# The second MLP's down products: three of four per slab by seven block products in place of eight, with the weight sums on GpSimd

## The reference, cut to what matters

```
def sqrelu_mlp(h, w1, w2):
    a = jax.nn.relu(h @ w1)          # h 256 x 2048, w1 2048 x 8192
    return (a * a) @ w2              # w2 8192 x 2048
...
x = x + mix                          # the S5 mixer with its gated output (tags gl, gg)
x = x + sqrelu_mlp(rmsnorm(x, norm_mlp[i]), mlp_w1[i], mlp_w2[i])
...
return rmsnorm(x, norm_final)
```

## Time and profile before

| | us |
|---|---|
| median of 3 runs | 2880.29 |
| lowest, highest | 2875.42, 2881.31 |
| span of the profiled execution | 2881.1 |
| PE busy in the span | 2841.2 |
| DVE busy | 1848.5 |
| ACT busy | 1408.0 |
| POOL busy | 374.1 |

### The profile page before, as it was taken

How to read it: one execution, slowest core, us unless ns; L and a number is a source line. 1 busy time by engine, 2 the same in 40 slices (tenths; PEclk the granted TensorE clock), 3 DMA queues, 4 the chain that set the end, 5 groups by cost and what they waited for, 6 DMA issues and landing times.

```text
span 2881.1 us, 46128 instructions
## 1 busy us (share of the span) xinstructions
PE 2841.2 (99%) x19454; PEld 2585.9 (90%) x19454; DVE 1848.5 (64%) x2543; ACT 1408.0 (49%) x1980; POOL 374.1 (13%) x420
## 2 busy tenths in 40 slices
PE   8999999999999999999999999989999999999998
PEld 8999988998899998999998899878889899988997
DVE  6998655776576665677665666677555555555555
ACT  5434645556555555444444445654545444444444
POOL 0000000000000000007883654122000000000000
PEclk9999999999999999999999999999999999999999
DMA  7555455552555555567776666586655555555553
GB/s 243 191 190 174 137 201 182 190 188 88 175 188 171 171 174 176 191 203 241 237 239 214 237 234 210 200 248 194 199 191 190 194 197 194 190 190 196 197 192 132
DMA packets 288047, 557.99 MB, mean 194 GB/s; under 512 B 25376, under 2 KB 35872, under 8 KB 287584
## 3 DMA queue, kind: packets, MB, share of 16 engines
q1 hardware_dynamic: 275328, 514.49, 54.3%
q0 software_dynamic: 5600, 22.78, 2.0%
q10 hardware_dynamic: 6912, 17.76, 1.8%
HBM read 530.87 MB, written 24.12 MB: 193 GB/s over the span
## 4 chain that ended last, share of the span: by engine, by line
PE 91%; DVE 4%; ACT 2%; DMA 1%; issue 1%; SPq 0%; ACTq 0%; POOL 0%; DVEq 0%
PE G L506 86%; PE T L506 3%; DVE WL L1714 1%; ACT WH L1103 1%; DVE Y L1722 1%; DMA FD<-s_k 1%; PE T L585 1%; DMA s_k<-VAR 1%; DVE XX L1714 0%; PE G L983 0%; ACT L1100 0%; ACT SC_e L1106 0%; DVE ZZ L2374 0%; DVE ST L1795 0%; DVE SC_e L1722 0%
## 5 line engine op out<-in xcount | busy, mean ns | idle before, releaser
L1714 DVE TENSOR_TENSOR WL<-RAW,WH 128x1024 fp32r<-128x1024 f32 (+1 forms) x948 | 1183.1, 1256 | 766.3 <-ACT WH L1103 756.6
L1103 ACT ACTIVATE WH<-RAW 128x1024 fp32r<-128x1024 f32 (+1 forms) x948 | 994.7, 1056 | 1027.7 <-PE G L506 1026.5
L506 PE MATMUL G<-A1h,WH 128*128 128x256 f32 (+1 forms) x2587 | 720.4, 280 | 3.1 <-DVE WL L1714 2.1
L506 PE MATMUL G<-A1l,WH 128*128 128x256 f32 x2560 | 712.9, 278 | 0.0
L506 PE MATMUL G<-A1h,WL 128*128 128x256 f32 x2560 | 711.5, 278 | 0.0
L506 PEld LDWEIGHTS G<-A1h,WH 128*128 128x128 f32 x2587 | 487.3, 189 | 7.0 <-DVE WL L1714 3.1
L506 PEld LDWEIGHTS G<-A1l,WH 128*128 128x128 f32 x2560 | 483.9, 189 | 0.4
L506 PEld LDWEIGHTS G<-A1h,WL 128*128 128x128 f32 x2560 | 482.9, 189 | 0.0
L506 PE MATMUL G<-WH,Bh 128*128 128x512 f32 x1024 | 399.3, 390 | 0.6 <-DVE WL L1714 0.6
L506 PE MATMUL G<-WH,Bl 128*128 128x512 f32 x1024 | 398.5, 389 | 0.0
L506 PE MATMUL G<-WL,Bh 128*128 128x512 f32 x1024 | 398.5, 389 | 0.0
(11 more groups left out here) (332 smaller groups left out, 3461.5 us busy)
## 6 DMA issues: line engine op xcount, KB each, us to landing
RAW<-in_mlp_w SPq DMA_DIRECT2D x256, 1024.0 KB, 5.3
RAW<-in_even_w_in SPq DMA_DIRECT2D x52, 1024.0 KB, 5.1
RAW<-in_a_w_in SPq DMA_DIRECT2D x48, 1024.0 KB, 5.2
RAW<-in_b_w_glu SPq DMA_DIRECT2D x32, 1024.0 KB, 5.2
RAW<-in_odd_w_in SPq DMA_DIRECT2D x20, 1024.0 KB, 5.1
RAW<-in_even_w_out SPq DMA_DIRECT2D x16, 1024.0 KB, 5.0
RAW<-in_odd_w_out SPq DMA_DIRECT2D x16, 1024.0 KB, 5.0
RAW<-in_a_w_out SPq DMA_DIRECT2D x16, 1024.0 KB, 5.0
```

The lines of the kernel that those rows point to most:

```text
L506: return e.matmul(out, lhsT, rhs, start=start, stop=stop, skip_group_check=True)
L1103: return e.activation(out, in_, ACT.Copy, scale=scale, bias=0.0)
L1714: return e.tensor_tensor(out, a, b, op)
```

## The change

```diff
+SEVEN = (0, 1, 2)
+PRODUCTS = ("21*11", "22*21", "D4*12", "D1*S2", "D2*S1", "D3*S3", "11*S4")
...
+    for s in range(9):
+        for i in range(2):
+            if s < 8:
+                weights(f"m1u{s}{i}", w1[1], 2048, 1024 * s + 512 * i, fm=True, steps=1)
+            if s > 0:
+                for k in (2 * i, 2 * i + 1):
+                    weights(f"m1d{s - 1}{k}", w2[1, 1024 * (s - 1):1024 * s], 1024, 512 * k, steps=1, seven=k in SEVEN)
...
+            for q, p in enumerate(PRODUCTS):
+                n = next(half)
+                if q % 2 == 0 and before is not None:
+                    e.wait_ge(*q_acc[before, q // 2])
+                e.wait_ge(*w_lo[n])
+                hi, lo = slot((WH, WHm), n), slot((WL, WLm), n)
+                Ah, Al = blocks(p)
+                o = TB[q // 2][:, 256 * (q % 2):256 * (q % 2) + 256]
+                for j in range(4):
+                    mm(o, Ah[:, j, :], hi[:, j, :], j == 0 and q % 2 == 0, False)
+                    mm(o, Ah[:, j, :], lo[:, j, :], False, False)
+                    m = mm(o, Al[:, j, :], hi[:, j, :], False, j == 3)
+                m.then_inc(*w_read.up(n))
+                step(STEPS[tag])
...
+        def seven(tag, k, first, sums):
+            for h, p in enumerate(PRODUCTS):
+                n = next(half)
+                while split[0] < min(n + RS, limit[0]):
+                    split_next()
+                if h in (2, 4, 6) and not first:
+                    add_products(tag, k, h // 2 - 1)
+                step(STEPS[tag])
+            if not first:
+                add_products(tag, k, 3)
+            if sums:
+                add_blocks(tag, k)
...
+            tt(v, v, TB[b][:, 0:w], ALU.add).then_inc(*q_acc.up((tag, b)))
...
+        def weight_sums(tag, s, before):
+            c = first_chunk[tag]
+            b11, b12, b21, b22 = (quarter(tag, b) for b in (11, 12, 21, 22))
+            S1, S2, S3, S4 = (as_tiles(TSUM[j]) for j in (1, 0, 2, 3))
+            for i in range(2):
+                e.wait_ge(*w_in[(c + i) % NR][c + i])
+            if before is None:
+                e.wait_ge(*x_up["gg3", 1])
+            else:
+                e.wait_ge(*w_lo[product(before, "D2*S1")])
+            tt(S2, b21, b22, ALU.add).then_inc(*t_sum.up((tag, 0)))
+            tt(S1, b12, b22, ALU.add).then_inc(*t_sum.up((tag, 1)))
+            if before is not None:
+                e.wait_ge(*w_lo[product(before, "11*S4")])
+            e.wait_ge(*d_l[s, 1])
+            e.wait_ge(*t_sum[tag, 1])
+            tt(S3, S1, b21, ALU.add).then_inc(*t_sum.up((tag, 2)))
+            e.wait_ge(*t_sum[tag, 2])
+            tt(S4, S3, b11, ALU.add).then_inc(*t_sum.up((tag, 3)))
...
+                if chunks[old][2]:
+                    tag = tag_of[first]
+                    e.wait_ge(*w_lo[product(tag, "D4*12" if old == first else "22*21")])
+                    e.wait_ge(*t_sum[tag, 3 if old == first else 2])
```

More of the change, by code:

```diff
@@ L280, in build_program, with weights @@
     turn = itertools.cycle((0, 2))
-    def weights(tag, w, K, n0, N=512, fm=False, first=0, steps=0, split=True):
+    def weights(tag, w, K, n0, N=512, fm=False, first=0, steps=0, seven=False):
         kts = K // 128
@@ L285, in weights @@
         first_chunk[tag], STEPS[tag] = len(chunks), steps
-        bank = next(turn) if split else 2
-        G_of[tag] = G[bank:bank + 2]
+        if not seven:
+            bank = next(turn)
+            G_of[tag] = G[bank:bank + 2]
         SHAPE[tag] = (kts, N, fm, [(first + k) % kts for k in range(0, kts, 4)])
         for k0 in SHAPE[tag][3]:
-            chunks.append((v[:, k0:k0 + 4, n0:n0 + N], (4, N), split))
+            chunks.append((v[:, k0:k0 + 4, n0:n0 + N], (4, N), seven))
     we, wo = t["even_w_in"][0], t["odd_w_in"][0]
@@ L946, in mlp, with second_mlp @@
                     for i in range(4):
[L947 to L955, removed]
-            finish()
+                        gemm(f"m0d{s - 1}{i}", Bh[o], Bl[o],
+                             None if i else (lambda kt, s=s: kt % 2 or e.wait_ge(*m_l[0, s - 1, kt // 2])))
+                        if s == 8:
+                            beside(norm_block("s", i, f"m0d7{i}"))
+            last()
+            finish()
+        def second_mlp():
+            before = None
+            for s in range(9):
+                for i in range(2):
+                    if s == 0 and i == 0:
+                        gemm("m1u00", A3h, A3l, a_ready("m1"), soon=lambda: rows("m1", TB[0]), at=4)
+                    elif s < 8:
+                        gemm(f"m1u{s}{i}", A3h, A3l)
+                    if s == 0:
+                        continue
+                    at = s // 8
+                    if i == 0:
+                        e.wait_ge(*m_l[1, s - 1, 1])
+                        e.wait_ge(*d_l[s - 1, 1])
+                    for k in (2 * i, 2 * i + 1):
+                        tag = f"m1d{s - 1}{k}"
+                        if is_seven(tag):
+                            seven(tag, at, before)
+                            before = tag
+                        elif (s, k) == (8, 3):
+                            gemm_by_tokens(tag, EH[at], EL[at])
+                        else:
+                            gemm(tag, EH[at], EL[at])
         def turn_c():
@@ L1526, in mlp, with second_highs @@
-                        if s == 8 and (l == 0 or i < 3):
-                            beside(norm_block(ph, i, f"m{l}d7{i}", Ah, gains, last if i == 3 else None))
+                        gemm(f"m0d{s - 1}{i}")
+                        if s == 8:
+                            beside(norm_block("s", i, f"m0d7{i}", Ah, gains, last if i == 3 else None))
+            finish()
+        def second_highs(s):
+            at = s // 7
+            for k in range(2):
+                if s and k == 0:
+                    e.wait_ge(*w_read[last_half(f"m1u7{1}" if at else f"m1d{s - 1}3")])
+                e.wait_ge(*m_sq[s, 2 * k + 1])
+                copy(EH[at][:, 4 * k:4 * k + 4, :], HS[:, 4 * k:4 * k + 4, :]).then_inc(*m_h.up((1, s, k)))
+                yield
+            if at:
+                for _ in range(units("m1d62") - 2):
+                    yield
+            for k in range(2):
+                e.wait_ge(*d_sum[s, k])
+                copy(DH[at][:, 2 * k:2 * k + 2, :], TSUM[2 + k][:, :].rearrange("p (a b) -> p a b", b=512)).then_inc(
+                    *d_h.up((s, k)))
+                yield
@@ L2218, in dve, with first_mlp @@
         norm_scale("m0", 3)
-        def mlp(l, ph, Ah, Al, gains, after=None):
-            Bh, Bl, RE, SQ = MLP[l]
+        def first_mlp():
             for s in range(9):
@@ L2435, in gains @@
             yield
-        mlp(1, "f", None, None, None, gains)
+        second_mlp(gains)
         for i in range(2):
```

369 lines of the change are left out of this document (280 added, 89 removed).

## The result

The changed kernel takes 3001.74 us in the median (2994.09 to 3004.0, 4 runs) against 2880.57 us (4 runs): ratio 1.0425, 95% interval [1.0408, 1.0442]. It is slower, as predicted, but by 121 us where 80 were predicted, and outside the range of 2912 to 2990. The profiled execution has a span of 3002.2 us.

What follows compares the result with a forecast made beforehand. PE was taken to bound the kernel, busy 2841.2 of 2881.1 us. 2881.1 + 32.4 (slabs 2 to 7) + 4.6 (slab 1) + 2.1 (last low parts) + 38.6 (end) + 3 (clock) = 2961.8, said as 2960; range 2912 to 2990.

Steps and rivals of the forecast that it cites:

- PE's saving: Block products: 1.36 us less matmul time for each of 24, -4.1 us per slab, whose PE time becomes 82.9.
- The lock: DVE's splits and POOL's sums exclude each other; in d1 PE's late units come in steps of 3.4 us, not 1.36.
- the sign that I named: In d0 and d1, splits with `TSUM` would average 2 us and more, in pairs with POOL's sums.
- The third to sixth split come late: P3 is 5.0 in place of 4.1: In d0, splits taking turns with POOL's sums delay PE's start of the fourth unit to 5.0 us.
- nobody waits for DVE: Read from the waits before the change: ACT waits for PE and DVE for ACT, so splitting keeps up.
- d2's sums run in u(s)1, whose units of 2.72 cover them; I find no stall there: The third block product's POOL sums fall in the up product before it and cost PE no stall.
- the seven pairs: d0 and d1 together: PE ends d1 at 28.6 us in place of 19.0, 9.5 us of stall.
- The end: From PE's start of d63 to the last matmul: 93.0 us in place of 54.4, +38.6.
- The clock: PE's clock may fall in the last 6.8 us of matmuls, behind `add_blocks`: between 0 and 6.8, taken as 3 us.
- as a rival, 28 in the pairs: Rival: the clock falls in each pair, some 4 us per slab, +28, 2989 us in all; 14%.
- packing is better: Rival: POOL's sums slip under adds and idle times; a slab costs 0 to +2, the end +25, 2913 us; 17%.
- The bound of 83 us of DVE and POOL: Per slab, mutually exclusive work: DVE's splits and low parts 51 us, POOL's sums 32, as much as PE's 82.9.

Runs made afterwards that it cites:

- run 1: Changed kernel with POOL's weight and token sums cut to 8 columns from the second block product on: 2882.9 us, ratio 1.003 to the kernel before.
- run 2: Changed kernel with POOL's sums replaced by memsets of the same tiles, which write but read nothing: 2877.36 us, ratio 1.0011 to the kernel before.
- run 6: Changed kernel where from slab 1 on ACT squares `RB` in place of `RM`, without waiting for `RM`: 2971.07 us, ratio 1.0317 to the kernel before.
- run 7: Changed kernel with the last group's products by eight blocks again and `add_blocks` moved to slab 6's products: 2960.57 us, ratio 1.0293 to the kernel before.
- run 8's last kernel: Changed kernel with only product 3 of slabs 0 to 6 by seven blocks, squares unmoved, last group by eight: 2875.17 us, ratio 0.9988.

## Why the prediction was right and where it was wrong

- **PE's saving** (-4.1 per slab): right to 0.8 us in the best slabs. With the reads gone a slab takes 83.7 or 85.1, for 82.9 (run 1). What the sum did not have is that a 256-column matmul is not always at 0.113 us: where it comes every 0.118, a block product takes 9.9 and saves 1.0 us, not 1.4.
- **The lock**: right in kind and size. It is POOL's reads (runs 1 and 2), and the alternation gives the predicted steps, about 3.3 us between PE's late units. Sums of POOL in six slabs, and the splits in the pair of s = 2, where 2.40 and 1.23 are the lengths alone:

```profile
L2731 POOL TENSOR_TENSOR TSUM<-RAW 128x1024 f32<-128x1024 f32 x36 | 115.1, 3216 | 232.5 <-DMA RAW<-in_mlp_w 112.2 <-issue 74.7 <-DVE WLm L1891 45.5
```
```profile
L1891 DVE TENSOR_TENSOR WLm<-RAW,WHm 128x1024 fp32r<-128x1024 f32 x6 | 15.4, 2585 | 0.0
L1891 DVE TENSOR_TENSOR WLm<-TSUM,WHm 128x1024 fp32r<-128x1024 f32 x8 | 11.1, 1423 | 1.6 <-ACT WHm L1220 1.6
```

  So the sign that I named, splits with `TSUM` of 2 us and more, was not there (1.42): the splits that meet the sums are mostly those of `RAW`.
- **"The third to sixth split come late: P3 is 5.0 in place of 4.1"** (P3 is PE's start of the fourth unit): wrong, 7.2. This is the step that failed. I let the first splits queue behind POOL's sum, but left out that DVE has `RM` and ACT the squares to do between the third and the fourth split of the next product. In the kernel before, the instructions in that place (`SQ`, `Bh`, `Bl`) lay under units of 2.72 us and kept no PE waiting, so I read past them; their own waits were in the view from which rows 5 were taken, so "nobody waits for DVE" held for PE alone:

```profile
ACT Bh L1103 <- DVE SQ L1722: 25.3, 31, 0.9
```

  Run 6 shows the price: 1.5 us in the pair, and 1.5 to 4.0 in d2, the lower clock included.
- **"d2's sums run in u(s)1, whose units of 2.72 cover them; I find no stall there"**: wrong, 2.5 to 4.9 us in each slab, 26.9 in all seven (93.5 for 7 x 9.52), for the same reason, and because d2's sums start 9.8 us into u(s)1 (I had taken about 8, as for d0's): the splits left over from the pair hold back the load of d2's second chunk (the fourth split of u(2)1, which frees its place, ends 4.4 us into it, not 2.6, and the sums start 5.3 us after). Units of 2.72 do cover the sums; what they don't cover is the last sum's end, and the fewer and shorter units behind it.
- **The sizes add up**: the seven pairs took 214.2 us for the 199.4 predicted (6 x 28.6 + 27.8), and the seven d2s 93.5 for 68.7 (7 x 9.52 + 2.1). That is 39.6 of the 40.8 us missed in the slabs.
- **The end**: right, and not by luck, for its landmarks came where they were put: `DL` held d70 until 15.3 us, as predicted to a tenth, d70's last split for the next product ended at 38.6 (predicted 39), the last split of all at 87.1 (86). 95.7 us in place of 93.0 and 3 for the clock. Runs 1 and 7 show that 25 of the +41 are POOL's reads and that it comes with the block products of the last slab; that the missing cover of an up product makes it so dear is argued from the order, not shown.
- **The clock**: I gave it 3 us in the last product, and, as a rival, 28 in the pairs. Windows of d2 in two slabs and of the pair in three:

```profile
2390.61:2404.45 13.84, 11.53 (x86) 11.33 (x85) 12.13 (x12) 8.21 (x9) 4.52 (x3) 0.88 0.45 153
...
2687.01:2699.13 12.12, 9.81 (x86) 9.61 (x85) 10.48 (x10) 8.21 (x9) 2.80 (x2) 1.00 0.52 173
```
```profile
2437.21:2467.71 30.50, 21.07 (x170) 19.75 (x169) 28.86 (x22) 15.63 (x16) 13.90 (x5) 1.00 0.41 138
...
2731.89:2762.55 30.66, 24.15 (x170) 23.12 (x169) 29.02 (x23) 15.62 (x16) 13.91 (x5) 0.83 0.41 137
```

  In the pair a lower clock costs nothing (30.50 at full speed, 30.66 at a mean of 0.83), for DVE is the bound. In d2 it costs 1.7 us (12.12 against 13.84), in five of seven slabs: some 8 us, part of the 26.9. So it fell where I had not looked, in a product whose stall was itself the left-out chain; without the chain's wait (run 6) all pairs and d2s are at 1.00. In the last product it averaged 0.90 over 17.3 us, which I estimate at 1.7 us, for the 3.
- **The rival "packing is better"** asked for a slab of at most +2. With all three block products none came near it. The bound of 83 us of DVE and POOL was never reached, since waits and order leave gaps.

About 12 of the 40.8 us missed ahead of d63 remain beside run 6's 28.7. In run 6 the pairs still take 202.7 us for 199.4 and the d2s 73.6 for 68.7, and three u(s)1 take 22.6 in place of 21.8, by slower matmuls and not by a wait; in the changed kernel all seven take 21.8. What makes the rest stays open.

## What to carry to other kernels

When units get shorter, follow every instruction that stands between two splits on each engine, also those that show no wait now: a chain across two engines (here DVE, ACT, DVE, 4.2 us) that was covered by units of 2.72 us is not covered by as many of 1.36. Work on GpSimd that reads SBUF is not free beside VectorE instructions with two SBUF inputs: add the busy times of both as one resource, and then place them against the waits, since the sum is only the lower bound. And put the step with the least slack behind the longest cover: with one product per slab by seven blocks, the place behind an eight gave 9.9 us for it, the place behind an up product 10.5, and moving the chain 11.4. The other place moved POOL's sums too, so how much of this is the cover alone was not separated.

## What the hardware showed that I had not expected

- TensorE's granted clock fell for short times within a product. PE ran at full speed to 2394.8, waited, and then went on; windows of d12, in pieces:

```profile
2390.60:2394.80 4.20, 4.20 (x38) 4.08 (x36) 3.67 (x3) 1.10 (x2) 1.39 (x1) 1.00 0.16 37
...
2397.15:2400.60 3.45, 3.41 (x20) 3.41 (x21) 3.45 (x4) 2.63 (x3) 0.00 (x0) 0.65 0.94 355
```

  After a wait of 2.3 us the matmuls from 2397.41 to 2398.11 came every 0.12 us and those from 2398.24 on every 0.213, the lower level (1.2 GHz), until 2401.5. In other slabs the same wait was followed by full speed throughout (12.12 us, above).
- At a granted clock of 1.00 the 256-column matmuls come at one of two paces, each held for tens or hundreds of matmuls: 0.113 us from start to start, or 0.118. Two rows of PE in d3 of run 8's last kernel:

```profile
2384.34 0.28 PE L578 MATMUL T<-WHm,EH 128*128 128x256 f32 x1
2384.46 0.28 PE L578 MATMUL T<-WLm,EH 128*128 128x256 f32 x1
```

  All 84 matmuls of that product are 0.117 to 0.119 apart (84 x 0.118 = 9.9 us), the up product after it is at 0.113 again. In run 2 the slower pace holds in u(s)1 of six slabs in a row (22.6 us) and in d2 of five of them (9.9), in the changed kernel through no u(s)1. What sets it is open.
- Token sums of 128x512 took as long as 2.2 us each beside the splits (12 of `TSUM<-HS`, mean 2222 ns). I had reckoned 1.15, half of 2.40. They lie in d3, where nothing waits for them except in the end.
